# A recurrent trunk step on one core: samples' residual and normed x as four stacked quarters, router logits four times, statistics by tile at the end

## The reference

```python
x   = layernorm(x)                                   # ln_in
h   = mixer(x)                                       # mLSTM | HGRN2, one in- and one out-projection
x   = layernorm(alpha * x + h)                       # ln1
logits = x @ w_router + b_router                     # 32 experts
top_v, top_i = top_k(logits, 4); gates = softmax(top_v)
y   = sum over the 4 experts of gate * (((up + 1) * glu) @ w_down + b_down)
x   = layernorm(alpha * x + y + per_layer_embedding) # ln2
```

## Time and profile before

| | |
|---|---|
| median of three runs | 1262.06 us |
| the profiled execution's own time | 1263.85 us |
| its span, first to last instruction | 1262.0 us |
| PE busy | 1166.6 us, 92% |
| DVE busy | 400.7 us, 32% |
| ACT, POOL busy | 178.2 us, 77.2 us |
| moved by DMA | 441.92 MB, 350 GB/s over the span |

### The profile page before, as it was taken

One profiled execution on the slowest core, in us unless ns is written; L12 is line 12 of the kernel. 1 busy time (PEld: TensorE's weight loads), 2 busy tenths in 40 slices (PEclk: granted clock), 3 DMA queues, 4 the chain that ended last, 5 costly groups with the idle time before them and its releaser, 6 DMA issues.

```text
span 1262.0 us, 13214 instructions
## 1 busy us (share of the span) xinstructions
PE 1166.6 (92%) x5599; PEld 483.0 (38%) x5599; DVE 400.7 (32%) x643; ACT 178.2 (14%) x321; POOL 77.2 (6%) x77
## 2 busy tenths in 40 slices
PE   3999999799999997899999999999999999998984
PEld 2777774643333332242333333332323232322221
DVE  6866423841223130112322222232323222214115
ACT  1253242411010110020101010100101010110001
POOL 3100141400101030000000000000000000000000
PEclk9999999899999998999999999999999999999987
DMA  9562111579999999999999999999999999999891
GB/s 313 176 180 67 67 68 67 208 300 420 421 421 421 422 420 386 421 422 421 416 422 421 421 421 421 406 422 420 421 420 421 420 422 412 422 421 413 370 420 55
DMA packets 70029, 441.92 MB, mean 350 GB/s; under 512 B 7824, under 2 KB 7856, under 8 KB 20816
## 3 DMA queue, kind: packets, MB, share of 16 engines
q1 hardware_dynamic: 65168, 425.52, 82.6%
q0 software_dynamic: 4800, 15.51, 3.7%
HBM read 436.28 MB, written 4.73 MB: 349 GB/s over the span
## 4 chain that ended last, share of the span: by engine, by line
PE 70%; DMA 19%; DVE 8%; ACT 2%; issue 1%; SPq 1%; DVEq 0%
PE ps L935 41%; DMA more<-in_w_up 11%; PE ps L543 9%; PE ps L919 5%; PE ps L871 3%; DVE y_s L1740 2%; PE ps L761 2%; DMA ring<-in_w_gate 2%; DMA more<-in_w_down 2%; DMA more<-in_w_gate 2%; PE ps L926 1%; PE ps L571 1%; DVE h_s L1738 1%; ACT hTe L1084 1%; DMA ring<-in_w_up 1%; PE ps L951 1%
## 5 line engine op out<-in xcount | busy, mean ns | idle before, releaser
L935 PE MATMUL ps<-ring,xTe 128*64 128x512 f32 x1536 | 357.4, 602 | 13.4 <-DMA ring<-in_w_up 9.1
L935 PEld LDWEIGHTS ps<-ring,xTe 128*64 128x64 f32 x1536 | 103.9, 136 | 242.0 <-issue 241.8
L1722 DVE TENSOR_TENSOR xs<-xs,ps 128x512 f32<-128x512 f32 (+1 forms) x128 | 70.5, 551 | 365.3 <-PE ps L919 364.7
L935 PE MATMUL ps<-ring,hTe 128*64 128x512 f32 x768 | 181.4, 613 | 4.5 <-DMA ring<-in_w_down 4.5
L935 PE MATMUL ps<-more,xTe 128*64 128x512 f32 x512 | 117.1, 598 | 6.0 <-DMA more<-in_w_up 5.8
L543 PE MATMUL ps<-xT,ring 128*128 128x288 f32 x448 | 116.6, 417 | 1.0 <-PE ps L543 0.6
L935 PEld LDWEIGHTS ps<-ring,hTe 128*64 128x64 f32 x768 | 51.7, 139 | 119.7 <-issue 119.4
L543 PEld LDWEIGHTS ps<-xT,ring 128*128 128x128 f32 x448 | 85.8, 196 | 25.6 <-issue 2.3
L919 PE MATMUL ps<-y_s,GT 128*128 128x512 f32 (+1 forms) x256 | 81.8, 518 | 1.2 <-ACT y_s L1084 1.2
L1738 DVE TENSOR_SCALAR h_s<-ps 128x512 f32<-128x512 f32 x32 | 21.8, 681 | 159.3 <-PE ps L935 159.3
L1754 DVE TENSOR_TENSOR ple<-ple,ps 128x512 f32<-128x512 f32 (+1 forms) x64 | 35.3, 551 | 105.0 <-PE ps L871 90.8
(11 more groups left out here) (344 smaller groups left out, 796.2 us busy)
## 6 DMA issues: line engine op xcount, KB each, us to landing
ring<-in_w_gate SPq DMA_DIRECT2D x96, 1024.0 KB, 10.7
ring<-in_w_up SPq DMA_DIRECT2D x96, 1024.0 KB, 12.1
ring<-in_w_down SPq DMA_DIRECT2D x96, 1024.0 KB, 13.6
more<-in_w_gate SPq DMA_DIRECT2D x32, 1024.0 KB, 12.2
more<-in_w_up SPq DMA_DIRECT2D x32, 1024.0 KB, 12.1
more<-in_w_down SPq DMA_DIRECT2D x32, 1024.0 KB, 13.8
ring<-in_w_in SPq DMA_DIRECT2D x28, 512.0 KB, 6.1
ring<-in_w_out SPq DMA_DIRECT2D x8, 512.0 KB, 5.0
```

What stands on the lines that cost most here:

```text
L935: last = mm(ps[64 * q:64 * q + 64, bank0 + half, :], lhs(k, q), wide(t)[:, k % 2, half * 512:(half + 1) * 512], start=False, stop=k == KT - 1)
L1722: last = tt(xs[0:r, i, c], xs[0:r, i, c], new, ALU.add)
```

## The change

The samples' residual moves from `xs[0:32, 2, :]` to `xq` of 128 partitions x 256 columns: quarter q of a row's columns lies on partitions 32q to 32q+31. `x1q`, `ple[:, 2, 0:256]` and the gains and biases of the norms (`ln_q`) have the same form. What was an instruction on 32x1024, or four on 32x256, becomes one on 128x256. A row's statistics are then spread over four partitions: `spread_stats` puts each partition's `bn_stats` into the slot of its quarter, PE adds them over the four quarters (`row_stats`, one product with the new constant `CF_SAME`), and `bn_aggr` reads the four sets from PSUM.

```diff
-                sp.dma_start(xs[0:r, i, :], x_src[i]).then_inc(S[f"x_in{i}"], 16)
+                    for q, x in enumerate(quarters(x_src[2])):
+                        sp.dma_start(xq[q * NS:(q + 1) * NS, :], x).then_inc(S["x_in2"], 16)
+                    for n, v in enumerate(("ln_in_g", "ln_in_b")):
+                        for q in range(4):
+                            sp.dma_start(ln_q[q * NS:(q + 1) * NS, n, :],
+                                         a[v][q * QW:(q + 1) * QW].partition_broadcast(NS)).then_inc(S["lnq_in"], 16)
...
+            def row_stats(n):
+
+                pe.wait_ge(S["lnq_ok"], n)
+                mm(ps[:, STAT_BANK, 0:24], cf[:, CF_SAME:CF_SAME + P], lnq[:, :, :].rearrange("p q s -> p (q s)"),
+                   start=True, stop=True).then_inc(S["lnq_mm"], 1)
...
+            def spread_stats():
+
+                tt(lnq[:, :, :], lns[:, 2, 0:1, :].to_broadcast([P, 4, 6]),
+                   cf[:, CF_QUARTER:CF_QUARTER + 4].unsqueeze(2).to_broadcast([P, 4, 6]), ALU.mult).then_inc(S["lnq_ok"], 1)
```

```diff
-                nc.gpsimd.tensor_tensor(out, out if q else x1[0:r, i, :], p, ALU.subtract).then_inc(S["rest_ok"], 1)
-
-            for i in range(3):
+                nc.gpsimd.tensor_tensor(natural(out), natural(out if q else x1[:, i, :]), by_row(xb[:, i, q, :]),
+                                        ALU.subtract).then_inc(S["rest_ok"], 1)
+
+            for i in range(2):
...
+            def copy_sample_rows():
+                for n in range(2):
+                    act.wait_ge(S["row_mm"], n + 1)
+                    f(by_row(xb_s[:, :])[:, 64 * n:64 * n + 64, :], natural(ps[0:3 * NS, ROW_BANKS[n], :]),
+                      ACT.Copy).then_inc(S["part_ok"], 1)
...
+            def rest_of_samples(q):
+                dve.wait_ge(S["partq_ok"], q + 1)
+                tt(rest_q[:, :], rest_q[:, :] if q else x1q[:, :], xbq[:, q, :], ALU.subtract).then_inc(S["restq_ok"], 1)
```

```diff
             project_out(2)
+            transpose_normed(1)
+            row_stats(2)
             route(0)
-            transpose_normed(1)
+            transpose_normed(2)
             route(1)
+            route(2)
+            prompt_ranks()
+            sample_rows()
+            sample_ranks()
             prompt_states_b()
-            transpose_normed(2)
-            route(2)
+            prompt_states_a()
...
+            select(0)
+            rest_of_samples(0)
+            select(1)
+            rest_of_samples(1)
+            select(2)
...
-            add_shares(NPAIR - 1)
+            add_shares(NPAIR - 1, tile_stats)
```

More of the change, by code:

```diff
@@ L21 @@
 NS = NSEQ * TS
+QW = D // 4
 NT = NP + NS
@@ L103, in trunk_step, with quarters @@
     x_src = [a["x_prompt"][0, 0:P, :], a["x_prompt"][0, P:NP, :], a["x_sample"].rearrange("b t d -> (b t) d")]
+    def quarters(rows):
+        return [rows[:, q * QW:(q + 1) * QW] for q in range(4)]
     p_src = [a["p_prompt"][0, 0, 0:P, :], a["p_prompt"][0, 0, P:NP, :],
@@ L493, in _ @@
             pool.wait_ge(S["ln3_in"], 32)
+            pool.wait_ge(S["lnq_next"], 16 * 16)
         @block.tensor
@@ L1076, in _ @@
                             combine_unit(n, GT[0])
+            row_stats(3)
         @block.scalar
@@ L1334, in _, with tile_stats @@
             nc.vector.memset(eps[:, 2:3], 1.0).then_inc(S["setup"], 1)
+            def tile_stats(i, done=None):
+                x = tokens(i)
+                for q in range(2 if i < 2 else 1):
+                    last = nc.vector.bn_stats(lns[:, i, q, :], x[:, q * 512:(q + 1) * 512] if i < 2 else x)
+                    (done or step)(last)
+            def spread_stats():
+                tt(lnq[:, :, :], lns[:, 2, 0:1, :].to_broadcast([P, 4, 6]),
+                   cf[:, CF_QUARTER:CF_QUARTER + 4].unsqueeze(2).to_broadcast([P, 4, 6]), ALU.mult).then_inc(S["lnq_ok"], 1)
@@ L1360, in norm_apply @@
+                step(stt(x, x, mv[:, i, 0:1], g, ALU.subtract, ALU.mult))
+                dve.wait_ge(S["ln_std"], n)
+                step(nc.vector.reciprocal(mv[:, i, 3:4], mv[:, i, 2:3]))
+                stt(normed(i) if 4 <= n < 7 else x, x, mv[:, i, 3:4], b, ALU.mult, ALU.add).then_inc(S["x_norm"], 1)
                 dve.wait_ge(S["x_norm"], n)
             def norm(i, n):
+                tile_stats(i)
+                if i == 2:
+                    spread_stats()
                 norm_stats(i, n)
@@ L1646, in mixer_residual @@
             def mixer_residual(i):
-                r = TILES[i][1]
-                for half in range(2):
-                    dve.wait_ge(S["out_mm"], 2 * i + half + 1)
-                    for new, c in columns(i, half, out_bank(i, half)):
-                        last = stt(xs[0:r, i, c], xs[0:r, i, c], ALPHA, new, ALU.mult, ALU.add)
-                    last.then_inc(S["r1_ok"], 1)
+                if i == 2:
+                    dve.wait_ge(S["out_mm"], 6)
+                    stt(xq[:, :], xq[:, :], ALPHA, ps[:, 4, 0:QW], ALU.mult, ALU.add).then_inc(S["r1_ok"], 2)
+                else:
+                    for half in range(2):
+                        dve.wait_ge(S["out_mm"], 2 * i + half + 1)
+                        for new, c in columns(i, half, out_bank(i, half)):
+                            stt(xs[:, i, c], xs[:, i, c], ALPHA, new, ALU.mult, ALU.add).then_inc(S["r1_ok"], 1)
                 dve.wait_ge(S["r1_ok"], 2 * i + 2)
@@ L1858, in _ @@
                         add_shares(j + NPAIR)
+                dve.wait_ge(S["cb_added"], extra * 5 + 5 * NPAIR)
+                for i in range(3):
+                    tile_stats(i, lambda last: last.then_inc(S["stats_anew"], 1))
+                dve.wait_ge(S["stats_anew"], 5)
+            spread_stats()
             dve.wait_ge(S["ln3_in"], 32)
-            dve.wait_ge(S["cb_added"], extra * 5 + 5 * NPAIR)
             for i in range(3):
```

255 lines of the change are left out of this document (149 added, 106 removed).

## The result

| | before | after |
|---|---|---|
| median | 1261.93 us | 1278.66 us |
| span of the profiled execution | 1262.0 us | 1277.6 us |
| ratio, 95% interval | | 1.0129 (1.0112 to 1.0147) |

Each median is of four executions (the 1262.06 above is of the first three). The change makes the kernel 16.7 us slower; 5.1 us faster was forecast. The two spans differ by 15.6 us, and three stretches add up to it. The weights' stream starts 14.04 us later (274.42 in place of 260.38). From there to DVE's first addition of the last pair it takes 983.74 us where it took 981.13 (1241.51 less 260.38): 2.61 lost. From that addition (1258.16) to the end it takes 19.44 in place of 20.49: 1.05 gained.

A forecast was written before the change was run, and what follows sets the result against it. The experts' weights stream over DMA was taken as the bound, so only time ahead of and behind it counts: 0.9 + 2.9 - 0.6 + 1.9 = 5.1 us gained, 1262.06 to 1257.0, range 1252.0 to 1263.0.

The forecast's parts named there:

- ACT: 1.06 if it costs nothing: Middle, ahead of the samples' x_norm: ACT's conversion with scattered output priced at 1.7 us, 1.06 if scattering is free.
- Head and middle: Everything ahead of the first expert product: 0.9 us gained in the head, 2.9 us from second norm to first product.
- The price of POOL's read: Middle: POOL's subtraction with scattered input priced at 2.13 us, as if scattered reading were free; 3.4 as upper bound.
- The first rival: Middle: POOL's scattered read costs 3.4 us, first product 0.5 late, 1.7 gained in total, 1260.4 us; chance 0.24.
- DVE waits for POOL: Middle, selection: DVE instructions with two SBUF inputs wait for POOL's state products; of 4.5 us gained, 4.0 given back.
- the second rival: Middle: DVE's tensor_tensor does not wait for POOL, pick at 238.8, 9.3 gained in total, 1252.8 us; chance 0.20.
- The pick within 0.1 us: Middle: the samples' pick forecast at 243.0, or 242.1 with the head's 0.9 taken off; 0.5 us of gain remain.
- States ahead of the gather: Middle, pick to first product: all state products stand ahead of the gather on PE, 6.1 us, then gather and copies 3.9.
- The third rival: Middle: states ahead of the gather at the low clock make it slower, 4.4 lost there, 1264.3 us; chance 0.12.
- Stream: Experts' weights stream: no saving, and 256 KB more for the quarters of ln2's gain and bias, 0.6 us lost.
- Head: Start of the kernel, samples' first norm and transposes: first projection near 23.5 instead of 24.42, 0.9 us gained.
- Tail: Behind the last products: cheaper additions, statistics hidden beside PE, branch bare at 0.5, three extra issues; 1.9 us gained.

The follow-up runs named there:

- the last experiment: The best kernel so far with the last norm's bn_stats back behind all additions: 7.16 us from first addition to end of the samples' bn_stats, against 6.70.

## Why the prediction was wrong

It was wrong in one step: "ACT: 1.06 if it costs nothing, 1.7 if it costs what it cost DVE (2.04/1.28); the access is the same one, so 1.7." The access was not the same. DVE's row writes f32, ACT's new instruction bf16, and the ratio was carried from one engine and one width to another and then used as the upper bound. It measured 4.75. The width is what failed, more than the engine: ACT's own f32 write with a step of 512 bytes took 1.96, 1.8 times its time in order, where DVE's ratio was 1.6. The trace of before had no row for a bf16 write with a step, on any engine; the honest bound upward was open, and with six such instructions in the one queue that also holds the norms' square roots, it was the term to doubt.

- **Head and middle.** Forecast 3.8 gained, measured 14.0 lost. With the conversions in order it is 2.7 gained, and with that price alone the kernel before takes 1.0130 of its time. So the mechanism, its place and its size are shown. The 1.1 that remain lie behind the pick: PE is at the samples' ranks 0.15 late and takes 1.0 for ranks at a clock of 0.50 where 0.35 was priced from rows at 1.00, the states take 0.3 more.
- **The price of POOL's read.** 2.13 was taken, 2.86 measured, 3.4 the bound; worth 2.0 us from the first square root to the bias. By the 50% of the Trainium skill (page GPSIMD Engine Reference, section Performance pitfalls for Q7 kernels) it would have been 3.2, an estimate; the trace has 34% more. The first rival's own sum is 0.35 too high: from a pick at 246 its terms give 256.35, not 256.7.
- **DVE waits for POOL.** Right, and the second rival falls: `rest_q` and `oneh` have two operands in SBUF and last until POOL is done (2.96 and 1.94 where they take 0.42 and 0.29 alone). The prediction speaks of three such long rows in the kernel before and names two, 3.72 and 1.79.
- **The pick within 0.1 us, with all in order.** In part luck. The forecast let the samples' second rest, cast and `oneh` wait for POOL. In that trace it is tile 1's cast and `oneh` and the second rest that wait, and the samples' own selection behind them meets nothing, since POOL is done at 240.14 (DVE, then POOL):

```profile
235.20 1.22 DVE L1773 CAST top_f<-top_i 128x8 f32<-128x8 uint32 x1
236.45 1.93 DVE L1774 TENSOR_TENSOR oneh<-cf,top_f 128x128 f32<-128x128 f32 x1
...
238.71 1.71 DVE L1781 TENSOR_TENSOR rest_q<-rest_q,xbq 128x256 f32<-128x256 f32 x1
```

```profile
234.27 2.12 POOL L493 TENSOR_TENSOR rests<-rests,xb 128x1024 f32<-128x1024 f32 x1 [3.53 <-ACT xb L1156]
236.35 3.79 POOL L505 TENSOR_TENSOR T<-V,cf 32x1024 f32<-32x1024 f32 x2
```

- **States ahead of the gather.** 6.1 was forecast, 6.4 measured; the gather 4.0 for 3.9. The third rival, slower by this order, named a real cost, since 2.1 to 3.1 us come back when one group moves ahead; it is not what made the kernel slower, which the kernel with ACT in order shows.
- **Stream.** 0.6 was forecast for the bytes, 2.6 measured in the one trace, 1.7 in the mean of all. The missing term is the price of small broadcasts, 1.1; the rest is what executions differ.
- **Head.** 0.67 gained for 0.9 (23.75 in place of 24.42), but that is not shown: the first projection starts between 23.29 and 25.18 in the eleven traces with this head.
- **Tail.** 1.05 gained for 1.9. The additions and statistics took what the sum had (6.70 us for 6.74), though the waits for PE that were to hide both tiles' statistics are hardly there (the last experiment). From the samples' `bn_stats` to the end of the last aggregate the sum had 1.45 us; it takes 2.7. The branch that had been hidden under additions costs 1.53 us bare, not 0.5, and PE's round trip for the samples' statistics another 0.51. The last four transfers came 0.4 cheaper than priced:

```profile
1264.43 0.43 DVE L1419 BATCH_NORM_STATS2 lns<-xq 128x6 f32<-128x256 f32 x1
1266.39 0.18 DVE L1424 TENSOR_TENSOR lnq<-lns,cf 128x24 f32<-128x24 f32 x1 [1.53 <-issue]
...
1267.29 0.27 DVE L1433 BATCH_NORM_AGGREGATE mv<-ps 128x2 f32<-128x24 f32 x1 [0.51 <-PE ps L565]
```

Without ACT's price the change gives 1.3 us of the forecast 5.1, within what can be told from no change. By that one trace 1.1 are missing in front of the first product, 1.9 in the stream and 0.85 in the tail.

## What to carry to other kernels

When a permutation moves from one instruction to another, price it by engine, by width of the element and by side; if no row has all three the same, the bound is open, and a kernel that runs this one line alone on top of the old code is the cheapest test there is. Put a permutation where f32 is read, or where two narrow elements stay neighbours, and never on the side where single bf16 are written. Look at what else stands in the queue of the engine that gets the work: here square roots of 0.3 us behind a conversion that nobody needed yet carried the delay to all others.

## What was not expected of the hardware

- ACT writes 128x1024 single bf16 at a step of 16 to 256 bytes in 4.74 to 4.82 us, pairs 256 bytes apart in 1.10, f32 512 bytes apart in 1.96; it reads f32 with a step of 32 bytes in 2.06 to 2.08.
- Eight broadcasts of a 1 KB row to 32 partitions each bring the rate from 423 to 349 GB/s while they land, at a full share of the DMA engines.
- Taking away DVE's waits for POOL in the selection brought the pick 1.1 us and the first product nothing: with PE at a clock of 0.50, the routing became the bound, and the products behind the pick took longer.
